# Softmax scaling of plain heads on VectorE, with evacuations and turns one slot later

## The reference

```
# MIX: 4 mixers of 4 heads each, 64 columns a head: neighbourhood, differential, GQA and MLA attention
sc = einsum(q, k) * scale (+ bias);  p = softmax(sc);  o = einsum(p, v)
# differential: a = softmax(s1) - lam * softmax(s2);  o = a @ v
mix = concatenate([a_out, b_out, c_out, d_out]) @ w_o
# SWA: 16 query heads on 4 key heads, window of 128 tokens, a learned sink per head
probs = softmax(concatenate([scores, sink_col]))[..., :-1];  out = (probs @ v) @ w_o
# FOX: 16 heads, causal, with a forget gate
s = q @ k.T * hd ** -0.5 + lc[:, None] - lc[None, :];  p = softmax(where(mask, s, -inf));  out = (p @ v) @ w_o
# GLA: gated linear attention in chunks of 64 tokens, no softmax
```

## Time and profile before

| | us |
|---|---|
| median of 3 runs | 1906.06 (1905.43 to 1907.14) |
| the profiled execution, its own time | 1905.94 |
| its span in the trace | 1904.2 |
| TensorE busy | 1839.6 (97%) |
| VectorE busy | 1348.1 (71%) |
| ScalarE busy | 1004.2 (53%) |
| GpSimd busy | 78.5 (4%) |

### The profile page before, as it was taken

How to read it: one execution, slowest core, us unless ns; L and a number is a source line. 1 busy time by engine, 2 the same in 40 slices (tenths; PEclk the granted TensorE clock), 3 DMA queues, 4 the chain that set the end, 5 groups by cost and what they waited for, 6 DMA issues and landing times.

```text
span 1904.2 us, 33674 instructions
## 1 busy us (share of the span) xinstructions
PE 1839.6 (97%) x13104; PEld 1662.2 (87%) x13104; DVE 1348.1 (71%) x2158; ACT 1004.2 (53%) x1614; POOL 78.5 (4%) x98
## 2 busy tenths in 40 slices
PE   8999999999999998999999999999999999989998
PEld 8868999986899986899989789998979998869997
DVE  6758888775888876887877588886555556766555
ACT  7775334767533477533364453346864335764333
POOL 3003000000000000000000000003400000000000
PEclk9999999999999998999999999999999999999999
DMA  8538988533788842688853278885335554325552
GB/s 308 183 118 251 350 314 308 189 133 119 286 324 308 307 167 70 254 328 311 324 216 134 91 299 331 306 309 212 141 136 199 180 195 166 121 101 200 185 190 88
DMA packets 62058, 416.57 MB, mean 219 GB/s; under 512 B 9008, under 2 KB 9200, under 8 KB 13312
## 3 DMA queue, kind: packets, MB, share of 16 engines
q1 hardware_dynamic: 56016, 401.33, 57.0%
q0 software_dynamic: 5936, 13.79, 2.5%
HBM read 413.90 MB, written 3.19 MB: 219 GB/s over the span
## 4 chain that ended last, share of the span: by engine, by line
PE 83%; DVE 7%; ACT 7%; issue 2%; DVEq 1%; ACTq 1%; DMA 0%; SPq 0%
PE psu L533 35%; PE psy L701 18%; PE psy L595 6%; PE psy L587 5%; PE psu L550 4%; PE psy L641 4%; PE psy L574 2%; ACT work L839 2%; PE psu L781 2%; DVE wlo L951 1%; ACT work L851 1%; PE psy L664 1%; DVE x L1221 1%; PE pso L767 1%; PE psm L801 1%
## 5 line engine op out<-in xcount | busy, mean ns | idle before, releaser
L942 ACT CAST whi<-raw 128x2048 fp32r<-128x2048 f32 (+1 forms) x281 | 536.2, 1908 | 598.9 <-PE psu L533 398.7
L951 DVE TENSOR_TENSOR wlo<-raw,whi 128x2048 fp32r<-128x2048 f32 (+5 forms) x306 | 646.8, 2115 | 270.0 <-ACT whi L942 269.1
L533 PE MATMUL psu<-hlo,whi 128*128 128x256 f32 x1920 | 536.0, 279 | 0.0
L533 PE MATMUL psu<-hhi,wlo 128*128 128x256 f32 x1920 | 535.9, 279 | 0.0
L533 PE MATMUL psu<-hhi,whi 128*128 128x256 f32 x1920 | 535.9, 279 | 0.0
L533 PEld LDWEIGHTS psu<-hhi,whi 128*128 128x128 f32 x1920 | 360.9, 188 | 2.3
L533 PEld LDWEIGHTS psu<-hlo,whi 128*128 128x128 f32 x1920 | 360.9, 188 | 2.3
L533 PEld LDWEIGHTS psu<-hhi,wlo 128*128 128x128 f32 x1920 | 361.0, 188 | 0.0
L1153 DVE CUSTOM_DVE_ANT_0 ada_raw<-ada_raw,cvec 128x1024 f32<-128x1024 f32 x192 | 227.0, 1220 | 2.8 <-DMA ada_raw<-ada 2.8
L701 PE MATMUL psy<-whi,ahi 128*128 128x512 f32 x528 | 210.2, 398 | 0.0
L701 PE MATMUL psy<-wlo,ahi 128*128 128x512 f32 x528 | 207.9, 394 | 0.0
(11 more groups left out here) (342 smaller groups left out, 2893.5 us busy)
## 6 DMA issues: line engine op xcount, KB each, us to landing
raw<-wts SPq DMA_DIRECT2D x280, 1024.0 KB, 4.8
ada_raw<-ada SPq DMA_DIRECT2D x96, 1024.0 KB, 4.9
gain<-gate_rows POOLq DMA_DIRECT2D x8, 512.0 KB, 4.0
dense_bias<-rel_bias POOLq DMA_DIRECT2D x32, 64.0 KB, 10.3
nab<-dense_bias SPq DMA_DIRECT2D x2, 1024.0 KB, 7.6
ada_raw<-fox_rows POOLq DMA_DIRECT2D x4, 512.0 KB, 12.3
cb<-cst POOLq DMA_DIRECT2D x1, 1408.0 KB, 9.4
cb<-cst SPq DMA_DIRECT2D x1, 1056.0 KB, 10.1
```

Source lines behind the costliest of these rows:

```text
L533: last = mm(psu[:, bank, cc * SEQ:(cc + 1) * SEQ], a[:, cols], h[:, kt, :], start=(kt == 0 and j == 0), stop=(kt == KT - 1 and j == 2))
L942: nc.scalar.copy(whi[:, part_of(c), 0:n], raw[:, slot_of(c), 0:n]).then_inc(hi_done, 1)
L951: last = nc.vector.tensor_tensor(wlo[:, part_of(c), cols], raw[:, slot_of(c), cols], whi[:, part_of(c), cols].bitcast(f32), ALU.subtract)
```

## The change

Three things are changed for the heads that are not pair heads (12 in each MIX layer, 16 in each SWA layer and in FOX).

1. The scaling of the probabilities is done by VectorE: `act_normal` is gone and `dve_roots` multiplies in place behind the reciprocal, with a drain in between. The semaphore `r_ready` is gone; `pn_ready` is announced by VectorE.
2. `dve_roots` stands behind the maximum in the slot, in place of ahead of it. The evacuation of a value product stands at the head of the next slot, except for the last head of a layer. `divide_first` is dropped.
3. A group is turned one slot later than the table says (`rounds`), except for group 7. This holds for ScalarE and VectorE. TensorE's order isn't touched.

```diff
--- before.py
+++ after.py
@@ -75,6 +75,11 @@
     def turned(self, h):
         k = self.begin.get(h - 2)
         return k if k is not None and k < self.early else self.later(h - 3)
+
+    def rounds(self, h):
+
+
+        return [m for at, m in self.turn.items() if at == (h if m == 7 else h - 1)]
 
     def value(self, h):
         k = self.begin.get(h - 3)
@@ -265,7 +270,6 @@
         pt_ready = sem("pt_ready")
         o_done = sem("o_done")
         o_evac = sem("o_evac")
-        r_ready = sem("r_ready")
         pn_ready = sem("pn_ready")
         mix_ready = sem("mix_ready")
         gq_sum = sem("gq_sum")
@@ -841,16 +845,6 @@
                                                 accum_out=psum_[:, k % 4, t:t + 1])
                 last.then_inc(p_ready, 1)
 
-        def act_normal(act, I0, items, plan, h):
-
-
-            k = plan.score(h - 1)
-            if k is not None and items[k]["pair"] is None:
-                act.wait_ge(r_ready, plain_no(I0, items, k) + 1)
-                for t, span in enumerate(spans(items[k])):
-                    last = nc.scalar.activation(prob[:, k % 3, span], prob[:, k % 3, span], ACT.Copy, scale=rsum[:, k % 4, t:t + 1])
-                last.then_inc(pn_ready, 1)
-
         def dve_roots(dve, I0, items, plan, h):
 
 
@@ -860,7 +854,11 @@
                 if items[k]["sink"] is not None:
                     nc.vector.tensor_tensor(psum_[:, k % 4], psum_[:, k % 4], esink[:, k % 4], ALU.add)
                     nc.vector.drain()
-                nc.vector.reciprocal(rsum[:, k % 4], psum_[:, k % 4]).then_inc(r_ready, 1)
+                nc.vector.reciprocal(rsum[:, k % 4], psum_[:, k % 4])
+                nc.vector.drain()
+                for t, span in enumerate(spans(items[k])):
+                    last = nc.vector.tensor_scalar(prob[:, k % 3, span], prob[:, k % 3, span], rsum[:, k % 4, t:t + 1], None, ALU.mult)
+                last.then_inc(pn_ready, 1)
 
         def dve_divide(dve, I0, items, plan, k):
 
@@ -903,10 +901,9 @@
                                                       ALU.add, ALU.min, nmax[:, k % 4, t:t + 1])
             last.then_inc(max_ready, 1)
 
-        def dve_steps(dve, I0, items, plan, h, g, divide_first=False):
-            dve_roots(dve, I0, items, plan, h)
-            k = plan.value(h)
-            if k is not None and divide_first:
+        def dve_steps(dve, I0, items, plan, h, g):
+            k = plan.value(h - 1)
+            if k is not None and items[k]["pair"] is None and k < len(items) - 1:
                 dve_divide(dve, I0, items, plan, k)
             k = plan.score(h)
             second = None
@@ -918,12 +915,12 @@
                     dve_negated(dve, I0, items[k], k, score_at(plan, k))
                     second = k + 1 if pair else None
             k = plan.value(h)
-            if k is not None and not divide_first:
+            if k is not None and (items[k]["pair"] is not None or k == len(items) - 1):
                 dve_divide(dve, I0, items, plan, k)
             if second is not None:
                 dve_negated(dve, I0, items[second], second, score_at(plan, second))
-            if h in plan.turn:
-                m = plan.turn[h]
+            dve_roots(dve, I0, items, plan, h)
+            for m in plan.rounds(h):
                 dve_turn(dve, m, g, psu[:, 1, 0:SEQ] if plan is MIX and m < 2 else columns(plan, m))
 
 
@@ -1384,7 +1381,6 @@
                 if j is not None and j < 11 and i == 0:
                     evac(j)
                 act_copy(act, I0, items, MIX, h)
-                act_normal(act, I0, items, MIX, h)
                 act_exp(act, I0, items, MIX, h)
                 if j is not None and j < 11 and i == 1:
                     evac(j)
@@ -1429,8 +1425,7 @@
                     nc.scalar.activation(gs[:, 1, 0:8], gs[:, 0, 0:8], ACT.Ln, bias=epsc[:], scale=1.0 / HD)
                     nc.scalar.drain()
                     nc.scalar.activation(gs[:, 2, 0:8], gs[:, 1, 0:8], ACT.Exp, scale=-0.5).then_inc(sub_std, 1)
-                if h in MIX.turn:
-                    m = MIX.turn[h]
+                for m in MIX.rounds(h):
                     if m < 2:
                         act_turn(act, l, C1_O, m, l, psu[:, 1, 0:SEQ], m_tr, 2 * l + m + 1)
                     else:
@@ -1808,7 +1803,6 @@
                 if j is not None and j < 6 and i == 0:
                     evac(j)
                 act_copy(act, I0, items, SWA, h)
-                act_normal(act, I0, items, SWA, h)
                 if SWA_HEADS.get(h + 1, 0) == 4:
                     turned(4)
                 act_exp(act, I0, items, SWA, h)
@@ -1816,8 +1810,7 @@
                     evac(j)
                 if SWA_HEADS.get(h, 2) < 2:
                     turned(SWA_HEADS[h])
-                if h in SWA.turn:
-                    m = SWA.turn[h]
+                for m in SWA.rounds(h):
                     act_turn(act, DEPTH1, c0 + 6, m, g, columns(SWA, m), o_evac, I0 + 2 * m + 2)
                 if h == 23:
                     act_table(ACT.Sqrt)
@@ -1831,7 +1824,6 @@
             for h in range(FOX.slots):
                 j, _ = FOX.ended(h)
                 act_copy(act, I0, items, FOX, h)
-                act_normal(act, I0, items, FOX, h)
                 act_exp(act, I0, items, FOX, h)
                 if j is not None and 1 <= j < 13:
                     act.wait_ge(unit_mm, unit_no(DEPTH1, c0 + j) + 1)
@@ -1844,8 +1836,7 @@
                     else:
                         dst = fold(f_v, NT, D)[:, :, grp * 256:(grp + 1) * 256]
                         nc.scalar.copy(dst, fold(src, NT, 256)).then_inc(bank_free, 1)
-                if h in FOX.turn:
-                    m = FOX.turn[h]
+                for m in FOX.rounds(h):
                     act_turn(act, DEPTH1, c0 + 13, m, g, columns(FOX, m), o_evac, I0 + 2 * m + 2)
                 if h == 28:
                     act_table(ACT.Sqrt)
@@ -1952,7 +1943,7 @@
             items = heads_swa(n)
             rc, rsn = tabs(*CB2["rope_c"], 256), tabs(*CB2["rope_s"], 256)
             for h in range(SWA.slots):
-                dve_steps(dve, I0, items, SWA, h, g, divide_first=SWA_ROPE.get(h - 1, 0) >= 3)
+                dve_steps(dve, I0, items, SWA, h, g)
                 if h in SWA_ROPE:
                     r = SWA_ROPE[h]
                     nc.vector.drain()
```

## The result

The changed kernel takes 1919.34 us (median of 4, 1917.35 to 1920.16), the kernel before 1905.74 (1904.84 to 1907.14) beside it. The ratio is 1.0069 with a 95% interval of 1.0052 to 1.0087: slower by 13.6 us. The forecast was 1913.6, the range 1900 to 1921.

The account below looks back on a forecast made before the run. TensorE, busy 97% of the span, was taken as the bound, so only its idle time counts: 1905.94 - 11.9 (SWA) + 12.6 (MIX turns) + 7.0 (MIX clock) = 1913.6 us, range 1900 to 1921.

Parts of the forecast that it names:

- MIX, the turns a slot later: MIX slots 25 to 31: TensorE waits for low parts of groups turned later; 6.3 us a layer, 12.6 for both.
- The four waits named: TensorE's waits for low parts at slot 25's transpose and slots 27, 30, 31: about 3.6, 2.8, 1.8 and 3.1 us.
- X + 3.82: Earliest start of a MIX slab quarter needing a group turned one slot ahead; X is that slot's scores starting, in us.
- Y + 0.68: Old start of slot 31's quarter after scores start at Y, in us; forecast to move to Y + 3.82, +3.1.
- MIX, the early part: Early MIX: three TensorE waits (1.77, 1.75, 0.82 us) go, but VectorE's chain lets slot 25's transpose start only 0.8 us earlier.
- The clock in MIX: New TensorE waits in MIX bring two more low-clock spells a layer: 3.5 us each layer, +7.0 for both, bounds 0 and 12.
- the rival in which the clock doesn't fall: MIX's new waits bring no lower clock: 1906.6 us, no difference from before; chance 0.24.
- SWA: Two SWA layers: less TensorE idle time and some clock regained, 11.9 us gained, bounds 6 and 13.
- four waits that were to be left in the second layer: Second SWA layer: TensorE waits at an evacuation 1.15, head-group rotation 0.8, weight casts and low parts 1.3 and 1.05 us.
- no wait over 1.5 us: Expected sign in the profile after: no TensorE wait in the SWA windows longer than 1.5 us.
- VectorE as the bound: Rival: VectorE's added 10 us per SWA layer fall on the chain and nothing is gained there: 1925.5 us, chance 0.12.
- Turns in SWA and FOX cost nothing: Turns one slot later have a slot or more to spare in SWA; FOX forecast 0, bounds -0.3 and +1 us.

Follow-up runs that it names:

- Experiment 10: Changed kernel, but in MIX the late casts and low parts of groups 0 to 4 open their slot instead of closing it: 1888.96 us.
- Experiment 11: Changed kernel with 28 and 22 unread matmuls filling two TensorE waits (slots 25 and 27) in each MIX layer: 1907.2 us.
- experiment 4: Kernel before, with only the scaling moved to VectorE right behind the reciprocal; reciprocal ahead of the maximum, evacuation and turns in old slots: 1915.27 us.
- 7: Kernel of experiment 1, but sum, reciprocal and scalings stand ahead of the maximum as before; evacuation and turns stay: 1908.42 us.
- experiment 5: Kernel of experiment 1, but ScalarE does the scaling as before; VectorE only takes the reciprocal, behind the maximum: 1919.37 us.
- experiment 1: Changed kernel, but groups 0 to 4 of MIX are turned in the table's own slots again: 1886.53 us.
- 8: Kernel of experiment 1, but every evacuation is back at the end of its own slot: 1887.63 us.
- 9: Kernel of experiment 1, but every evacuation is in its own slot and every turn of every layer in the table's slot: 1888.46 us.

## Why the prediction was right, and where its parts were not

The direction, the range and the main mechanism held, and the time was 5.7 us off: the clock in MIX is 3.3 us of this, idle time in MIX 1.4, SWA 0.6 and FOX 0.45. Point by point:

**MIX, the turns a slot later.** Right, and the largest term. Forecast +6.3 us of idle time a layer, measured +7.4 and +6.6. The four waits named are 10.5 us, where the forecast had 11.3; what made the sum larger lies in the early part. The X + 3.82 of the prediction fits slot 27: its scores start at 107.10, and 110.93 is X + 3.83. In slot 30 it is 3.81, in slot 31 3.62, and the forecast took the whole shift of the quarter from Y + 0.68, 3.1 us, for a wait, though TensorE is busy with the scores until Y + 1.03. Experiment 10 confirms that the chain from scores to low part is what counts, since the same slot with the turn at its head gives nearly all of it back.

**MIX, the early part.** Right in its result, -0.8 us, by luck; its parts were not. Counted from the start of the layer, the transposes of slot 25 start 0.6 us earlier in the first layer and 1.3 in the second. But only two of the three waits went. That for `rows` grew from 0.82 to 2.05 us (0.83 to 1.68 in the second layer), as TensorE now comes to it sooner, so idle time up to the transposes rose by 1.1 and 0.4 us. What made up for it is the clock: its mean in this stretch was 0.91 and 0.92 before and is 0.99 in both layers now, which the forecast didn't count. It also missed that the wait at the transposes wasn't VectorE's work alone but the late turn of group 0: with the turns back it is gone in the first layer and 1.50 us in the second, and the layers gain 3.6 and 4.3 us. The forecast's list of what hangs on the late turns should have begun at slot 25.

**The clock in MIX.** Mis-sized. Forecast +3.5 us a layer (two spells of 3.4 us), measured +5.1 and +5.2 of busy time for the same matmuls. Two spells more came, as forecast. The step that failed is the length of a spell, 3.4 us, taken from two places of the kernel before: behind two long waits a few us apart one lasted about 10 us. The spell of 6.8 us at 748, which was in the trace before, would have warned of it. The bound of 12 for both layers held (10.3). Experiment 11 shows the cause; the rival in which the clock doesn't fall, at 1906.6, is out.

**SWA.** The sum was right, -11.9 against -11.3, the explanation in part. Of the four waits that were to be left in the second layer (1.15, 0.8, 1.3 and 1.05) four are left, of 1.14, 0.56, 1.28 and 0.93 us. In the first layer the gain is 1 us short, and the "no wait over 1.5 us" of the prediction failed, since one wait of TensorE for a maximum grew from 2.30 to 3.57 us: ahead of that maximum VectorE had a low part and two long sums (L1153, 1.22 us each) in a row before, and now has the scalings and a turn in front of them. The prediction named both steps, the maximum ahead of the reciprocal and ScalarE's shorter chain, but not that each needs the other; the expectation of experiment 4 then put most of the gain on the shorter chain and fell. The next table shows that neither half gains anything by itself:

| | scaling on ScalarE | scaling on VectorE |
|---|---|---|
| reciprocal ahead of the maximum | 1906 (before) | 1915.3 (experiment 4), 1908.4 (7) |
| reciprocal behind the maximum | 1919.4 (experiment 5) | 1886.5 (experiment 1) |

Experiments 1, 5 and 7 stand on the same evacuations and turns, the kernel before and experiment 4 on the old ones. What moved evacuations and turns cost was measured only with the scaling on VectorE (1.1 and 0.8 us, experiments 8 and 9); that they cost no more with it on ScalarE was not tried. On ScalarE the scaling stands between copy and exponentials, so a later reciprocal delays them. On VectorE ahead of the maximum it delays the maximum. Only behind the maximum on VectorE does it run beside the exponentials and delay nothing. The sentence of the prediction that used this (the scaling "falls into time in which VectorE would wait") was right.

**VectorE as the bound.** Rejected: 5.1 us more of its busy time cost 2.2 to 2.5 us in a SWA layer, not all of it. VectorE's added busy time in the whole kernel is 40.7 us, where the forecast had some 45.

**Turns in SWA and FOX cost nothing.** Nearly: 0.45 us in FOX, and in SWA they are rather a gain of some tenths.

## What to carry to other kernels

When a step is moved to the next slot, ask what it then stands behind: the same step first in that slot and last in it differed here by 30 us, which is more than everything else in the change was worth. Moving an operation to another engine and moving it in the order are not two gains that add; here they lost 9 and 12 us by themselves and won 20 together, so the order must be laid out anew for the engine that gets the work. And a wait of the engine that sets the pace is to be priced with its clock: in MIX 14.0 us of added idle time came with 10.3 us of slower work.

## What the runs showed of the hardware

**Filling idle time pays.** 100 matmuls without use made the kernel 12 us faster; the granted clock stayed at 1.00 in the stretch of the first MIX layer where it had been 0.50.

**Scalings can take three times as long beside GpSimd.** In FOX, GpSimd builds tables in the first part of the stage. VectorE's pairs of scalings there, from its timeline after, two of them beside GpSimd and two at or behind its end at 1371.2:

```profile
1363.08 1.60 DVE L860 TENSOR_SCALAR work<-work,rsum 128x128 f32<-128x128 f32 x2
...
1368.44 1.58 DVE L860 TENSOR_SCALAR work<-work,rsum 128x128 f32<-128x128 f32 x2
1371.05 0.55 DVE L860 TENSOR_SCALAR work<-work,rsum 128x128 f32<-128x128 f32 x2
1376.51 0.55 DVE L860 TENSOR_SCALAR work<-work,rsum 128x128 f32<-128x128 f32 x2
```

```profile
1365.65 2.97 POOL L516 TENSOR_TENSOR ada_raw<-ada_raw,work 128x512 f32<-128x512 f32 x1
1368.59 1.27 POOL L517 TENSOR_TENSOR nab<-nab,cb 128x512 f32<-128x512 f32 x1
1369.83 1.34 POOL L518 TENSOR_TENSOR ada_raw<-ada_raw,cb 128x512 f32<-128x512 f32 x1
```

In four slots of the changed kernel's FOX stage a pair takes 1.6 to 1.7 us in place of 0.55; one more pair beside GpSimd, at 1351.95, took 0.55. GpSimd's operations take 1.0 to 1.3 us, or about 3 where VectorE makes the low part of a weight unit beside them. The Trainium skill ("SBUF — State Buffer", section "Who interferes with whom") says that a VectorE operation in a mode with two ports and one of GpSimd exclude each other for their whole length. The four pairs agree with it; that the scalings ran in such a mode, the rows don't show. It is the likely reason why twice the scaling cost most in FOX (4.3 us), where in some slots VectorE had four such operations; that link was not tried by itself.
